# Stick-breaking attention by scanned sigmoids, with its transposes moved off TensorE, and the compression of mixer D moved in front of the second differential scores

## What is computed

```python
z = q @ k.T * scale
mask = kpos[None, :] < qpos[:, None]                 # strictly causal
log1m = where(mask, log_sigmoid(-z), 0.0)
between = cumsum(log1m, axis=3, reverse=True) - log1m
a = where(mask, exp(log_sigmoid(z) + between), 0.0)
o = a @ v
```

## Time and profile before

| | |
|---|---|
| median of three runs | 827.91 us (827.84 to 828.54) |
| the profiled execution | 828.2 us, of which span 826.4 us |
| TensorE products | 821.6 us busy, 99% of the span |
| TensorE weight loads | 673.7 us, 82% |
| VectorE | 559.7 us, 68% |
| ScalarE | 477.8 us, 58% |
| GpSimd | 293.7 us, 36% |

### The profile page before, as it was taken

The page is one execution under the profiler, slowest core; times in us unless marked ns, Lnnn a source line. Parts: engine busy times, 40 slices in busy tenths (PEclk is TensorE's granted clock), DMA queues, the critical chain, the costliest instruction groups (busy, mean ns, idle before and its releaser), DMA issues.

```text
span 826.4 us, 11044 instructions
## 1 busy us (share of the span) xinstructions
PE 821.6 (99%) x4050; PEld 673.7 (82%) x4050; DVE 559.7 (68%) x821; ACT 477.8 (58%) x715; POOL 293.7 (36%) x297
## 2 busy tenths in 40 slices
PE   9999999999999999999999999999999999999998
PEld 5888888888888888888888888888788888888886
DVE  5576889868865666655454688898697666666542
ACT  6886655785465554543457775567844645454441
POOL 0078784404303432320000889653061044323100
PEclk9999999999999999999999999999999999999999
DMA  9745877684558777785565556878745687877652
GB/s 332 271 138 178 222 230 219 182 247 131 203 178 229 199 230 212 223 221 183 167 203 195 162 192 192 224 222 210 223 153 178 206 214 218 230 223 212 215 184 71
DMA packets 119637, 167.76 MB, mean 203 GB/s; under 512 B 56608, under 2 KB 59040, under 8 KB 119328
## 3 DMA queue, kind: packets, MB, share of 16 engines
q1 hardware_dynamic: 119296, 166.79, 66.9%
q10 hardware_dynamic: 288, 0.27, 0.1%
HBM read 153.40 MB, written 1.05 MB: 187 GB/s over the span
## 4 chain that ended last, share of the span: by engine, by line
PE 98%; DMA 1%; issue 0%; SPq 0%; ACT 0%; DVE 0%
PE acc L732 91%; PE att L812 1%; PE att L895 1%; PE att L779 1%; PE att L886 1%; DMA w_raw<-in_w_in 1%; PE att L804 1%; PE acc L812 1%; PE att L853 0%; PE att L869 0%; PE att L908 0%; PE att L972 0%; PE att L963 0%; PE att L854 0%; PE att L839 0%
## 5 line engine op out<-in xcount | busy, mean ns | idle before, releaser
L1234 DVE TENSOR_TENSOR w_lo<-w_raw,w_hi 128x1024 fp32r<-128x1024 f32 (+1 forms) x276 | 365.4, 1337 | 147.1 <-ACT w_hi L996 144.6
L732 PE MATMUL acc<-w_hi,xt 128*128 128x512 f32 (+1 forms) x1728 | 432.3, 392 | 0.5 <-ACT xt L1019 0.3
L996 ACT ACTIVATE w_hi<-w_raw 128x1024 fp32r<-128x1024 f32 (+1 forms) x275 | 286.1, 1051 | 168.7 <-PE acc L732 159.1
L732 PEld LDWEIGHTS acc<-w_hi,xt 128*128 128x128 f32 x1728 | 319.0, 188 | 66.3 <-issue 1.3
L732 PE MATMUL acc<-w_lo,xt 128*128 128x512 f32 (+1 forms) x864 | 229.9, 388 | 0.0
L732 PEld LDWEIGHTS acc<-w_lo,xt 128*128 128x128 f32 x864 | 162.0, 188 | 32.9
L1485 POOL TENSOR_SCALAR small<-small 128x2 f32<-128x2 f32 (+4 forms) x14 | 10.4, 745 | 209.2 <-ACT sq_dump L1096 132.4
L1617 POOL COPY hid_t<-hid_halves_t 128x512 uint16<-128x512 uint16 x44 | 37.7, 885 | 94.3 <-DMA hid_halves_t<-hid_halves 80.0
L1608 POOL COPY hid_halves<-hid 128x512 uint16<-128x512 uint16 x44 | 45.6, 1064 | 65.2 <-DVE hid L1311 65.2
L1625 POOL TENSOR_TENSOR merged<-merged,prod 128x1024 f32<-128x1024 f32 x10 | 32.5, 3250 | 61.2 <-DVE prod L1283 60.3
L732 PE MATMUL acc<-w_hi,ht_hi 128*128 128x512 f32 x176 | 47.7, 390 | 0.0
(11 more groups left out here) (175 smaller groups left out, 723.5 us busy)
## 6 DMA issues: line engine op xcount, KB each, us to landing
w_raw<-in_w_ffn SPq DMA_DIRECT2D x88, 512.0 KB, 4.2
w_raw<-in_w_gate SPq DMA_DIRECT2D x64, 512.0 KB, 3.9
w_raw<-in_w_ffn_down SPq DMA_DIRECT2D x44, 512.0 KB, 4.0
w_raw<-in_w_in SPq DMA_DIRECT2D x39, 512.0 KB, 4.7
w_raw<-in_w_branch SPq DMA_DIRECT2D x16, 512.0 KB, 4.1
w_raw<-in_w_out SPq DMA_DIRECT2D x16, 512.0 KB, 3.3
bg<-in_b_gate SPq DMA_DIRECT2D x8, 512.0 KB, 5.4
w_raw<-in_w_in SPq DMA_DIRECT2D x8, 396.0 KB, 3.4
```

Of the source, the lines that this page charges most:

```text
L732: return pe.matmul(acc[bank0 + t][:, 0:N], x_part[:, k0 + k, t * P:(t + 1) * P], w_part[:, k, 0:N], start=first, stop=last)
L996: act.activation(w_hi[:, n % WR, :, 0:N], w_raw[:, n % RAW, :, 0:N], copy).then_inc(s_hi, 1)
L1234: dve.tensor_tensor(w_lo[:, n % WR, :, 0:N], w_raw[:, n % RAW, :, 0:N], w_hi[:, n % WR, :, 0:N].bitcast(F32), ALU.subtract).then_inc(s_lo, 1)
```

## The change

Mixer A is computed another way. The step `sm` for A stands once, at slot 9, with both pairs of heads: plain scores, not transposed, the second pair in an idle product bank. VectorE reads them with an additive mask into `eb`. ScalarE (`ssig`, slot 10) takes the sigmoid of -z into `za` and of z into `eb`. VectorE (`sscan`, slots 11 and 12) runs a scan from right to left over each map, which multiplies up sigmoid(-z) and is set to 1 at the start of each row of queries, and multiplies the shifted result into `eb` (`smul`, slots 12 and 13). GpSimd deals the weights into halves (slot 13), Sync issues two more DMA transposes, before the loads of chunks 21 and 22, and ScalarE joins them into `za` (slots 18 and 19). Mask products, cumulative products, softplus and its parts are gone, and so are the mask tensor and ScalarE's three copies of constants at slot 7.

Mixer B's power -1/2 moves from GpSimd to ScalarE (`brs`, slot 14) as an Ln and an Exp. `lambda` moves from slot 14 to 15. The second two score pairs move from slot 27 to 30, and with them `p`, the transpositions and the products with V to slots 30 to 37, and the output to 38.

Mixer D's compression of keys and values is one step in the bank TP at slot 30, copied by one ScalarE instruction; the sum over strips moves to slot 33 and uses the whole array (128 columns in place of 16). `kcprep` moves from 32 to 34; `kct` from 37 to 38, as a product over 128 rows with the identity in place of a transposition of 16 rows. The scores of the compressed branch move from 39 to 40.

```diff
-TURNS = [("C", 0), ("C", 1), ("D", 0), ("D", 1), ("D", 2), ("D", 3)]
-TURN_P = (43, 47, 52, 53, 55, 56)
+TURNS = [("A", 0), ("A", 1), ("C", 0), ("C", 1), ("D", 0), ("D", 1), ("D", 2), ("D", 3)]
+TURN_P = (21, 22, 43, 47, 52, 53, 55, 56)
...
-    "Ak": 7, "Az": (9, 14), "Asp": (9, 14), "Acum": (13, 17), "Apv": (21, 21), "Bq": 19, "Bk": 20,
-    "Bsm": (21, 21, 27, 27), "Bp": (21, 24, 27, 29), "Bpt": (24, 27, 29, 32), "Bpv": (27, 29, 33, 35), "Bo": 36,
+    "Ak": 7, "Asm": (9, 9), "ssig": 10, "sscan": (11, 12), "smul": (12, 13),
+    "Apdeal": (13, 13), "brs": 14, "Apjoin": (18, 19), "Apv": (21, 21), "Bq": 19, "Bk": 20,
+    "Bsm": (21, 21, 30, 30), "Bp": (21, 24, 30, 32), "Bpt": (24, 27, 32, 34), "Bpv": (27, 29, 35, 37), "Bo": 38,
...
-    "cbuild": 29, "ck": 31, "cks": 31, "cv": 31, "kcprep": 32, "kct": 37, "cr": 35, "cs": 39, "cp": 39,
+    "cbuild": 29, "ck": 30, "cks": 33, "kcprep": 34, "kct": 38, "cr": 35, "cs": 40, "cp": 40,
...
-    "Bp": 5.5,
+    "Bp": 5.5, "smul": 2, "Apdeal": 0.2,
```

On TensorE:

```diff
-                if kind == "z":
-                    for b in (S0, S1):
-                        pe.matmul(att[:, b, :].rearrange("p (s c) -> p s c", c=P)[:, 0:3:2, :], ident16,
-                                  mask_a.unsqueeze(1).to_broadcast([P, 2, P]), start=True, stop=False, skip_group_check=True)
...
-                for h in range(2):
-                    for i in range(2):
-                        b, part = S0 + h, sp_parts[:, h, i, :]
-                        pe.matmul(att[:, b, 0:384], tri_r[:, 0, :], part, start=False, stop=False, skip_group_check=True)
-                        mm = pe.matmul(att[:, b, P:2 * P], tri_r[:, 1, :], part[:, 256:384], start=False, stop=i == 1,
-                                       skip_group_check=True)
...
-                m, b = (0, S0) if step[0] == "ck" else (1, S1)
-                for j in range(0, CMP_STRIDE, 4):
-                    for i in range(4):
-                        mm = pe.matmul(att[32 * i:32 * i + 32, b, 0:HD], cblk[:, m, j + i, :], cw[:, m, j + i, :],
-                                       start=j == 0, stop=j == CMP_STRIDE - 4)
+                for m in range(2):
+                    for j in range(0, CMP_STRIDE, 4):
+                        for i in range(4):
+                            mm = pe.matmul(att[32 * i:32 * i + 32, TP, m * HD:(m + 1) * HD], cblk[:, m, j + i, :],
+                                           cw[:, m, j + i, :], start=j == 0, stop=j == CMP_STRIDE - 4)
...
-                            pe.matmul(att[0:16, TP, 0:HD], cst[:, C_REP:C_REP + 16], kpart[:, :], start=True, stop=True
+                            pe.matmul(att[:, TP, 0:HD], cst[:, C_REP:C_REP + P], kpart[:, :], start=True, stop=True
...
-                            pe.transpose(att[:, TP, 0:16], kcs[:, :, :], ident[0:16, 0:16]
-                                         ).then_inc(att_done.now(step), 1)
+                            pe.matmul(att[:, TP, 0:16], kcs[:, :, :].rearrange("p m d -> p (m d)"), ident[:, 0:16],
+                                      start=True, stop=True).then_inc(att_done.now(step), 1)
```

On ScalarE, VectorE and GpSimd:

```diff
+                elif kind == "ssig":
+                    act.wait_ge(read_dve.sem, read_dve.at(l, ("sm", ("A", 1))))
+                    act.activation(za[:, :, :], eb[:, :, :], ACT.Sigmoid, scale=-1.0).then_inc(s_zc, 1)
+                    act.wait_ge(s_zc, l + 1)
+                    act.activation(eb[:, :, :], eb[:, :, :], ACT.Sigmoid).then_inc(act_misc.now(step), 1)
+                elif kind == "brs":
+                    act.wait_ge(dve_misc.sem, dve_misc.at(l, ("prep", "B")))
...
+                    act.activation(rs[:, 0:n], ss[:, 0:n], ACT.Ln, scale=1.0 / DD, bias=epsb[:, 0:1]).then_inc(s_brs, 1)
+                    act.wait_ge(s_brs, l + 1)
+                    act.activation(rs[:, 0:n], rs[:, 0:n], ACT.Exp, scale=-0.5).then_inc(act_misc.now(step), 1)
...
+                elif kind == "sscan":
+                    dve.wait_ge(s_zc, l + 1)
+                    for h in (2 * a, 2 * a + 1):
+                        ins = dve.tensor_tensor_scan(out=za[:, h, ::-1], data0=za[:, h, ::-1], data1=restart[:, ::-1],
+                                                     initial=0.0, op0=ALU.mult, op1=ALU.max)
+                    settled(ins)
+                elif kind == "smul":
+                    dve.wait_ge(act_misc.sem, act_misc.at(l, ("ssig", None)))
+                    h = slice(2 * a, 2 * a + 2)
+                    dve.tensor_tensor(eb[:, h, 0:383], eb[:, h, 0:383], za[:, h, 1:384], ALU.mult
+                                      ).then_inc(dve_misc.now(step), 1)
...
-                            settled(rsqrt(rs[:, 0:n], ss[:, 0:n], d, half[:, 0:n]))
+                            if a == "B":
+                                pool.wait_ge(act_misc.sem, act_misc.at(l, ("brs", None)))
+                            else:
+                                settled(rsqrt(rs[:, 0:n], ss[:, 0:n], d, half[:, 0:n]))
```

More of the change, by code:

```diff
@@ L154, in steps @@
             put(PLAN["prep"]["BCD".index(mixer)], "prep", mixer)
-        for n in range(PAIRS[mixer] if mixer != "A" else 0):
-            put(PLAN[mixer + "sm"][n], "sm", (mixer, n))
         for n in range(PAIRS[mixer]):
-            for kind in {"A": ("z", "sp", "cum", "pv"), "B": ("p",)}.get(mixer, ("p", "pdeal", "pjoin", "pv")):
-                put(PLAN[mixer + kind][n], kind, n if mixer == "A" and kind != "pv" else (mixer, n))
+            for kind in {"A": ("sm", "pdeal", "pjoin", "pv"), "B": ("sm", "p")}.get(mixer, ("sm", "p", "pdeal", "pjoin", "pv")):
+                put(PLAN[mixer + kind][n], kind, (mixer, n))
         for m in range(MAPS[mixer]):
@@ L291, in reader_of @@
     kind, a = step
-    by_dve = kind in ("pair", "sm", "cs", "cv", "cr", "o")
+    by_dve = kind in ("pair", "sm", "cs", "cr", "o")
     return "dve" if by_dve else "act"
 BANK_STEPS = [s for s in ORDER if banks_of(s)]
-BANK_USES = {b: [s for s in BANK_STEPS if b in banks_of(s) and s[0] != "cum"] for b in range(4)}
+BANK_USES = {b: [s for s in BANK_STEPS if b in banks_of(s)] for b in range(4)}
 def e_of(step):
     kind, a = step
-    if kind == "z":
-        return (0, 1, 2, 3), ("cum", a)
     mixer, n = a
@@ L307, in e_of @@
     return (first, first + 1), ("pt" if mixer == "B" else "pdeal", (mixer, n))
-E_STEPS = [s for s in ORDER if s[0] in ("z", "sm")]
+E_STEPS = keys("sm")
 def pt_slots(step):
@@ L317, in pt_slots @@
         return 2 * (a[1] % 2), 2 * (a[1] % 2) + 1
-    return (2 * a, 2 * a + 1) if kind == "cum" else (a[1],)
-PT_USES = [[s for s in ORDER if s[0] in ("cum", "pt", "pjoin") and slot in pt_slots(s)] for slot in range(4)]
+    return (a[1],)
+PT_USES = [[s for s in keys("pt", "pjoin") if s[1][0] != "A" and slot in pt_slots(s)] for slot in range(4)]
 def pv_step(s):
-    if s[0] == "cum":
-        return ("pv", ("A", s[1]))
     return ("pv", s[1])
 def trunk_kernel(nc, x, x_t, w_in, w_gate, w_branch, w_out, w_ffn, w_ffn_down,
-                 norm_g, gains, lam, cmp_pe, cmp_w, b_gate, const, masks, out):
+                 norm_g, gains, lam, cmp_pe, cmp_w, b_gate, const, out):
     with ExitStack() as ctx:
@@ L363, in trunk_kernel @@
         end_big = top[0]
+        za = place("za", [P, 4, 384], F32, at=zg_at + 4 * D_MODEL)
+        turn_at = {"p_halves": (zg_at + 16 * D_MODEL, big), "p_halves_t": (zg_at + 22 * D_MODEL, big + 4 * IN_COLS + 16)}
+        p_halves, p_halves_t = ([place(f"{name}{2 * j + i}", [P, 2, 2, 384], U16, at=at + 12 * i * MIX)
+                                 for j, at in enumerate(starts) for i in range(2)] for name, starts in turn_at.items())
         xt_raw = place("xt_raw", [P, KT, SEQ], F32, at=zg_at + 16 * D_MODEL)
@@ L534, in turned, with p_buffer @@
             return 16 * NT * (l * len(range(what % 2, N_FFN, 2)) + what // 2 + 1)
+        def p_buffer(k):
+            return k if k < 2 else 2 + k % 2
         def p_turned(l, step):
@@ L873, in times_v @@
                 mixer, m = step[1]
[L874 removed]
+                src = ("pt" if mixer == "B" else "pjoin", (mixer, m))
                 ev = pjoined if src[0] == "pjoin" else read_act
@@ L1674 @@
     columns = lambda g: np.asarray(g).reshape(L, KT, P).transpose(0, 2, 1)
-    const, masks = constants()
     arrays = {
@@ L1688 @@
                    .reshape(L, P, 2, CMP_STRIDE, HD),
-        "b_gate": b_gate, "const": const, "masks": masks,
+        "b_gate": b_gate, "const": constants(),
     }
```

197 lines of the change are left out of this document (83 added, 114 removed).

## The result

The changed kernel takes 833.77 us (833.35 to 833.94, four runs) where the kernel before takes 827.88 (827.82 to 828.54): ratio 1.0069, 95% interval 1.0056 to 1.0082. The forecast was 824.7 and faster; the time is also beyond the range (820.3 to 828.8). The profiled execution has a span of 831.5 us against 826.4 of before.

What follows compares the result with a forecast made beforehand. The prediction took TensorE's work, 98% of the span, as the bound. Per layer 3.7 gained less 1.1 and 1.0 of waits gave 1.6, 3.2 in two layers: from 827.9 to 824.7 us, range 820.3 to 828.8.

Steps and rivals of the forecast that it cites:

- A's second pair of copies: GpSimd, ahead of B's preparation: two copies of 1.08, taken at 2.2 us, bounds 1.6 to 3.5.
- the 3.2 us of gain: Whole kernel: 3.7 less waits of 1.1 and 1.0 leaves 1.6 us a layer, 3.2 in two layers.
- TensorE, mixer A: Two mask-and-score excursions and two cumulative products, 5.08 us a layer, become one excursion of 1.75: gain 3.33.
- TensorE, mixers B and D: Moved scores and compression share an excursion, gain 0.15; compressed keys as a 128-row product, gain 0.23 us a layer.
- First new wait, slot 19: TensorE's transposition of B's queries waits for GpSimd's preparation, ending at 63.3 against arrival at 62.2: 1.1 us a layer.
- body: Main part of GpSimd's preparation for B before slot 19: taken at 11.2 us, best end 8.8, worst 11.8.
- The scan: VectorE's scans for mixer A: 1.7 us a pair, between 0.96 at elementwise rate and twice that.
- Second new wait, slots 32 and 34: TensorE waits for B's late second scores, through ScalarE and VectorE: 1.0 us a layer, bounds 0 and 2.5.
- the second: Rival: GpSimd's preparation at slot 19 decides, up to 3.9 us a layer, kernel slower at 830.3; chance 0.15.
- worst ends: Slot 19: scan 1.9, mutual slowing 0.9, copies 3.5, body 11.8; preparation ends at 66.1, a stall of 3.9 us.
- The third: Rival: gain eaten exactly, slots 32 and 34 take 2.5 us, slot 19 takes 1.1: 827.7 us; chance 0.13.
- Nothing waits: Rival: scan at elementwise rate or GpSimd at C's pace, so no new waits: 827.9 - 7.4 = 820.5; chance 0.24.

Runs made afterwards that it cites:

- the version of 825.42 us: Changed kernel with B's transposition one chunk later, the compression product behind the split in slot 30, D's compressed scores behind the gate's read in slot 40: 825.42 us.
- The first late deal: Changed kernel with GpSimd's four copies for A moved behind B's preparation, and A's transposes, joins, products with V and output split later: 830.57 us, ratio 1.0034.
- the best version: The version of 825.42 us with the transposition of B's second pair of maps moved to slot 28 and of its third map to slot 33: 824.70 us.
- the later transposition: Changed kernel with B's query and key transpositions, first scores and what hangs on them, and A's products with V, one chunk later: 831.97 us, ratio 1.0047.
- the compression's rank: Changed kernel with only the compression's rank moved from 1 to 3.5, so ScalarE makes chunk 32's high part first: 830.33 us, ratio 1.0028.
- the rank of slot 40: D's compressed scores put behind the gate's read in slot 40; not tried alone, part of the version of 825.42 us.

## Why the prediction was wrong

**Which step failed.** The sum priced a wait of TensorE at its length and had no term for the clock behind it, and it took A's second pair of copies at 2.2 us where they took 3.52. The two made the 3.2 us of gain a loss.

**TensorE, mixer A: right.** The gain was forecast as 3.33 a layer. From the start of chunk 12 to that of chunk 18 it takes 20.04 us before (42.64 to 62.68) and 16.32 after (42.50 to 58.82), and the longer excursion in slot 9 costs 0.38 more: 3.34. The A scores stand as one piece of 1.5 us where I put them. (The 0.66 at 140.64 in the earlier trace rows are D's scores, in slot 42, and not C's; C's, at 117.61 in the same view, are 0.66 too.)

**TensorE, mixers B and D: too high.** I gave 0.15 + 0.23 us. The compressed keys' transposition gave back 0.15: the chunk behind it took 5.57 in place of 5.71, and the transposition 0.13 in place of 0.16. But from the start of chunk 20 to that of chunk 46 the changed kernel takes 88.79 us (69.74 to 158.53) against 87.06 before (68.97 to 156.03). Of the 1.73 more, 1.22 are the wait of slot 32 and 0.5 the two small waits named below, which leaves nothing of the gain of 0.38. In the version of 825.42 us, from chunk 18 to chunk 46, it is 95.38 against 93.35: 2.03 more, of which the wait is 1.10. What makes the remaining 0.9 was not isolated.

**First new wait, slot 19: the mechanism right, the size wrong.** Forecast 1.1, measured 2.87 and 2.80. Its terms, forecast and measured: the product done 49.9 and 50.09; logarithm and exponential done 50.5 and 51.1, hidden; second pair of copies **2.2 and 3.52**; body 11.2 and 10.8; end 63.3 and 64.44; TensorE's arrival 62.2 and 61.70, half a microsecond earlier as this execution started faster. The mis-sized term is the copies, 1.3 of the 1.8 us that were missing. The rest is VectorE's chain less the faster body: the product came 0.2 us later than in the sum although TensorE arrived 0.5 earlier. My upper bound for the copies was 3.5 (the longest copy of before took 1.76), and I took a value near the lower end though two low parts of VectorE were due just then. The first late deal shows the same copy at 0.82 with a one-input VectorE instruction beside it.

The Trainium skill, "SBUF — State Buffer", section "Who interferes with whom", says that a VectorE instruction with two inputs in SBUF contends with GpSimd's reads, and that one with at most one input, outside the two-port modes, does not. The traces agree: 1.49 to 1.82 us a copy beside low parts and scans, 0.82 beside a sum. With the copies at their dear end, 3.5, the forecast wait would have been 2.4.

**The scan** was taken at 1.7 a pair and is 1.80 alone, where the product over as many elements takes 0.96. The half throughput that the prediction quotes from the Trainium skill ("DVE: opcode table, instruction layouts, handler registers and perf-mode slots", section "Datapath and trigger behaviour") is borne out, with 1.9 by that rule. The pair beside the copies took 3.01, more than my upper bound of 1.9 and its 0.9 of slowing; the product was still done at 50.09, as the chain began 0.6 us earlier than I had it (41.13 for 41.7).

**The clock: missing from the sum.** I priced a wait at its length. In the profiled executions the granted clock fell to 0.50 behind five of the six waits of 2.8 to 2.9 us in slot 19, behind both of 5.7 and behind the two of 4.2 and 5.0 in slot 26; of the four of 2.1 to 2.4 in slot 32 it fell behind two, and behind the three of 1.9 it did not fall. It costs 3.2 us in the profiled execution of the changed kernel, and at most 1.9 in medians where the wait is filled. The slot-19 wait alone, with 3.5 us more than forecast over both layers, had already used up the 3.2 us of gain; the clock made the loss clear.

**Second new wait, slots 32 and 34.** Forecast 1.0 a layer, measured 1.22 in slot 32 and none in slot 34. The mechanism is as forecast up to the exponentials; the combination of the first pair took 2.03 us (106.90 to 108.93) and not the 1.26 of before. More than half of the wait goes with the order of the compression's copy and a high part on ScalarE. **Two that I missed**: C's keys' copy in slot 27 (about 0.3 us a layer, 1.1 once slot 19 is repaired), and 0.21 in slot 42, where D's scores need a bank whose reader now stands behind the compressed scores moved to slot 40.

**The rivals.** The one that decided was the second, and by more than its price: the wait and the clock together are 4.6 and 4.3 us a layer, over its bound of 3.9. (The worst ends given for it add up to 66.5 and not 66.1, so that bound should have been 4.3.) It was held unlikely because it needed slow copies and a slow body together; the copies were slow, the body was not, and the clock did the rest. The third, with 2.5 us in slots 32 and 34, did not come: they took 1.2. The second's threshold, 2.7 beside a wait of 1.0, was right, and a wait of 2.8 without the clock's fall would have left the kernel at about 828: 827.9 - 7.4 + 5.7 + 2.0. "Nothing waits", 820.5, was never reached: the best version stands at 824.7 with 1.5 to 1.8 us of waits left.

**Sum as it came out.** In the profiled executions: -6.7 (A) + 5.7 (slot 19) + 3.2 (clock) + 2.4 (slot 32) + 1.0 (the rest of slots 20 to 46) - 0.5 (start-up) = 5.1, from 826.4 to 831.5. Against the forecast of 824.7 the median is 9.1 us too long: 3.5 from slot 19, up to 3.2 from the clock, 1.0 from the two small waits, 0.8 from the gain in B and D that did not come, 0.4 from slot 32. The remainder, larger if the clock is taken at its price in medians, no trace shows.

## What to carry to other kernels

Before work of a full engine is shortened, list its next operands from the other engines with their margins: here slot 19 had 0.6 us of slack, and 3.3 us were taken out in front of it, so a repair of the schedule (the consumer one chunk later, 2.7 us) belonged into the change. Price a wait on TensorE with the clock that may fall behind it (here behind two of four waits of 2.1 to 2.4 us and five of six of 2.8 to 2.9), and a GpSimd copy that meets VectorE's two-input work at twice its length. And after each repair look for the next late operand: the later transposition and the compression's rank were worth 1.8 and 3.4 us by themselves, and 8.4 together with the rank of slot 40.

## What the runs showed that I had not expected

- An idle stretch of 2.87 us cost 1.6 us more in the chunk behind it. With the slot-32 wait reduced, filling it with twelve useless products made the kernel 1.9 us faster; with the slot-32 wait as it was, filling it gained nothing.
- The clock's fall is not the same in every execution: one kernel took 830.05 to 830.64 us in five of them and 831.8 to 831.9 in the two with the lower mean clock.
- The same GpSimd copy took 0.82 to 1.82 us and the same VectorE scan pair 1.80 or 3.01, by what the other engine was doing.
- Where VectorE too waits for the preparation, the GpSimd work that TensorE waits for is faster: four products in 2.77 us in place of 5.78.
- The logarithm and the exponential each had a table load of 1.28 us ahead of them (46.98 and 49.61).
